# The halves of the weights begin 64 bytes later in SBUF, except for the experts

## The reference

```python
def reference(x, mem, ...):
    x = first_block(x, mem, ...)      # layer 0: RWKV-7 + S5 mixer, memory attention, SwiGLU of 2816
                                      # layer 1: differential attention, memory attention,
                                      #          8 experts of 3584, the best 2 of each token
    return second_block(x, ...)       # twice: attention + gating + convolution, then a SwiGLU of
                                      #        2816 with a convolution over tokens

def swiglu(h, w_gate, w_up, w_down):
    return (jax.nn.silu(h @ w_gate) * (h @ w_up)) @ w_down
```

## The kernel before

| tensor | first byte | modulo 256 |
|---|---|---|
| `ring` | 0 | 0 |
| `w_hi`, `w_lo` | 27648, 44032 | 0 |
| `x_hi`, `x_lo`, `act_hi`, `act_lo` | 60416, 68608, 76800, 80896 | 0 |
| `mix`, `rstd`, and `y2_hi`, `y2_lo` in `mix` | 131456, 139648 | 128 |
| `arena` (148928) with `m_hi`, `m_lo`, `d_hi`, `d_lo`, `x2_hi`, `x2_lo`, `more_hi`, `more_lo`, `more_raw`, `more_x_hi`, `sel_t`, `y_hi` | multiples of 256 behind 148928 | 192 |

## Time and profile before

### The profile page before, as it was taken

The page is one execution under the profiler, slowest core; times in us unless marked ns, Lnnn a source line. Parts: engine busy times, 40 slices in busy tenths (PEclk is TensorE's granted clock), DMA queues, the critical chain, the costliest instruction groups (busy, mean ns, idle before and its releaser), DMA issues.

```text
span 2824.1 us, 43102 instructions
## 1 busy us (share of the span) xinstructions
PE 2673.2 (95%) x18156; PEld 2377.1 (84%) x18156; DVE 1921.0 (68%) x2040; ACT 1477.4 (52%) x1687; POOL 116.2 (4%) x112
## 2 busy tenths in 40 slices
PE   7778999998998999999998899999999999999998
PEld 5667999988897887888886678888888899999998
DVE  7885656656745445875447876588888678766877
ACT  5314554456643334664336655467777565446543
POOL 7251000000000000000000000000000000000000
PEclk9899999999998999999999999999999999999999
DMA  5102545543424545885546875589999535534553
GB/s 206 61 2 92 163 155 189 194 150 105 149 75 171 191 174 196 302 321 195 180 176 255 332 278 211 214 304 351 353 342 362 205 130 182 188 116 143 193 181 120
DMA packets 219856, 558.31 MB, mean 198 GB/s; under 512 B 8592, under 2 KB 167440, under 8 KB 176400
## 3 DMA queue, kind: packets, MB, share of 16 engines
q1 hardware_dynamic: 217584, 553.47, 55.2%
q10 hardware_dynamic: 2080, 2.10, 0.2%
HBM read 554.48 MB, written 1.05 MB: 197 GB/s over the span
## 4 chain that ended last, share of the span: by engine, by line
PE 80%; DVE 9%; ACT 4%; issue 2%; DVEq 2%; DMA 1%; POOL 0%; POOLq 0%; ACTq 0%; SPq 0%
PE ps L886 23%; PE ps L888 23%; PE ps L887 22%; DVE w_lo L3508 2%; DVE w_lo L1853 2%; PE ps L1701 1%; PE ps L1702 1%; DVE more_lo L3508 1%; PE ps L1678 1%; ACT arena L1822 1%; DVEq L2608 1%; PE ps L1721 1%; ACT w_hi L1837 1%; PE ps L924 1%; PE ps L1129 1%
## 5 line engine op out<-in xcount | busy, mean ns | idle before, releaser
L1853 DVE TENSOR_TENSOR w_lo<-ring,w_hi 128x1024 fp32r<-128x1024 f32 x362 | 447.4, 1252 | 254.2 <-ACT w_hi L1837 248.2
L1837 ACT ACTIVATE w_hi<-ring 128x1024 fp32r<-128x1024 f32 x362 | 379.8, 1058 | 371.8 <-PE ps L888 356.2
L3508 DVE TENSOR_TENSOR w_lo<-ring,w_hi 128x2048 fp32r<-128x2048 f32 x168 | 384.0, 2289 | 173.7 <-ACT w_hi L1825 173.4
L886 PE MATMUL ps<-x_hi,w_hi 128*128 128x256 f32 x1600 | 459.3, 287 | 16.0 <-DVE w_lo L1853 7.9
L887 PE MATMUL ps<-x_lo,w_hi 128*128 128x256 f32 x1600 | 453.6, 284 | 0.0
L888 PE MATMUL ps<-x_hi,w_lo 128*128 128x256 f32 x1600 | 453.6, 283 | 0.0
L1825 ACT ACTIVATE w_hi<-ring 128x2048 fp32r<-128x2048 f32 x168 | 321.4, 1915 | 210.2 <-PE ps L888 135.8
L886 PEld LDWEIGHTS ps<-x_hi,w_hi 128*128 128x128 f32 x1600 | 308.0, 193 | 22.3 <-issue 16.3
L887 PEld LDWEIGHTS ps<-x_lo,w_hi 128*128 128x128 f32 x1600 | 308.3, 193 | 0.4
L888 PEld LDWEIGHTS ps<-x_hi,w_lo 128*128 128x128 f32 x1600 | 308.0, 192 | 0.0
L3508 DVE TENSOR_TENSOR more_lo<-ring,more_hi 128x2048 fp32r<-128x2048 f32 x84 | 192.4, 2290 | 87.6 <-ACT more_hi L1825 86.8
(11 more groups left out here) (451 smaller groups left out, 5832.4 us busy)
## 6 DMA issues: line engine op xcount, KB each, us to landing
ring<-moe SPq DMA_DIRECT2D x252, 1024.0 KB, 5.6
more_raw<-moe SPq DMA_DIRECT2D x84, 1024.0 KB, 5.2
ring<-ffn_w_up SPq DMA_DIRECT2D x44, 1024.0 KB, 5.1
ring<-ffn_w_down SPq DMA_DIRECT2D x22, 1024.0 KB, 4.8
ring<-xa_w_kv SPq DMA_DIRECT2D x16, 1024.0 KB, 5.3
ring<-w_in SPq DMA_DIRECT2D x16, 1024.0 KB, 5.5
ring<-da_w_qkv SPq DMA_DIRECT2D x12, 1024.0 KB, 5.1
ring<-ff_w_gate SPq DMA_DIRECT2D x11, 1024.0 KB, 5.4
```

What stands on the lines that cost most here:

```text
L886: mm(o, lhs[0], rhs[0], start=start, stop=False)
L1837: nc.scalar.activation(w_hi[:, half_slot(at, half), :], ring[:, s_, half * 1024:half * 1024 + 1024], ACT.Copy).then_inc(hi_ready, 1)
L1853: nc.vector.tensor_tensor(w_lo[:, i, :], ring[:, s_, half * 1024:half * 1024 + 1024], w_hi[:, i, :], ALU.subtract).then_inc(lo_ready, 1)
L3508: nc.vector.tensor_tensor(lo, raw_piece(n), hi, SUB).then_inc(piece_lo, 1)
```

## The change

Before `w_hi` a tensor of 16 columns (64 bytes) is put in and behind `w_lo` one of 240 columns (960 bytes). So `w_hi` and `w_lo` begin 64 bytes later, and all that follows 1024 bytes later. `even_hi` and `even_lo` are second names on the same memory, at the places where `w_hi` and `w_lo` lay before, and `split_piece`, which only the experts use, takes those.

```diff
@@ -340,8 +340,13 @@
         ring = sb("ring", [P, RING, KT * 288])
 
 
+        even_at = nc.sbuf_base
+        sb("odd_start", [P, 16])
         w_hi = sb("w_hi", [P, HALVES, 1024], F32R)
         w_lo = sb("w_lo", [P, HALVES, 1024], F32R)
+        sb("odd_end", [P, 240])
+        even_hi, even_lo = (nc.alloc_sbuf_tensor_at(f"even_w{i}", [P, HALVES, 1024], F32R, offset=even_at + 16384 * i)
+                            for i in range(2))
         x_at = nc.sbuf_base
         x_hi = sb("x_hi", [P, KT, S], F32R)
         x_lo = sb("x_lo", [P, KT, S], F32R)
@@ -490,7 +495,7 @@
         def split_piece(n):
             b = n % SPLITS
             if b < 2:
-                return [t[:, 2 * b:2 * b + 2, :].rearrange("p a n -> p (a n)") for t in (w_hi, w_lo)]
+                return [t[:, 2 * b:2 * b + 2, :].rearrange("p a n -> p (a n)") for t in (even_hi, even_lo)]
             return [t[:, b - 2, :] for t in (more_hi, more_lo)]
```

## The result

The change makes the kernel faster by 0.5%: 2815.32 us (median of 6 runs, 2804.52 to 2820.6) against 2827.85 us for the kernel before, timed beside it (6 runs, 2825.61 to 2831.57), ratio 0.995, 95% interval 0.9938 to 0.9961. The predicted 2802.5 us was 13 us too low; the range held. The six times lie 16 us apart (2820.6, 2815.04, 2813.66, 2815.59, 2815.96, 2804.52), those of before 6 us. The profiled execution is the slowest of the six, 2820.6 us, with a span of 2818.9 us and a clock of 0.978 as before.

A forecast was written before the change was run, and what follows sets the result against it. PE was taken as the bound (busy 95%), through the spacing of split-product matmuls. Gains of 36.5 us less losses of 13.3 us made 23.2 us off 2825.76 us: 2802.5 us, range 2787 to 2819.

The forecast's parts named there:

- Addresses matter at all: Split products on PE: where tiles begin sets matmul spacing, about 6.6 ns; rival "nothing at all", 2826 us, chance 0.04.
- Distance modulo 256: Split products: first byte streamed minus first byte loaded, modulo 256, sets spacing: 0 gives 120 ns, 192 113.4, 64 118.
- 118 ns everywhere: Rival: the new pairs run like w with m; gains 12.3 us, losses 13.3, 2826.8 us, no change; chance 0.10.
- `x` and `act` with `w` in the second block's feed-forwards at 113.4 ns, 20.9 us: Second block's two feed-forwards: distance 0 to 192 takes 3168 matmuls from 120.0 to 113.4 ns, gaining 20.9 us.
- slower rhythm in part: Rival: long feed-forward runs at distance 192 fall into 118 ns; one gives 2809.5 us, both 2816.5; chance 0.12.
- Distance 128 at 120 ns: m, d, x2 with w and w with m move to distance 128, taken at 120 ns: losses of 13.3 us.
- Gains in the first feed-forward and the first memory attention: Outside the second block's feed-forwards: act in the first feed-forward gains 3.5 us, 1920 matmuls of x elsewhere 11.5 us.
- Splits and experts unchanged: Splits on DVE and ACT stay at 2289 and 1915 ns, the experts' stretch at 1380 us; nothing counted.
- PE waits for nothing new: Second block's feed-forward: with PE at 179 us DVE is busy 83% and keeps ahead, so no new wait.
- The Trainium skill's rule: TensorE waits for no other SBUF user and weight loads take no read bandwidth, so addresses would be free; forecast followed rows instead.

The follow-up runs named there:

- e8: Kernel before with the arena alone moved 64 bytes later, so all pairs of split products have distance 0: 2828.01 us, ratio 0.9997.
- e4: The change with w_hi and w_lo 128 bytes later instead of 64 (x and act with w at distance 128): 2827.64 us, ratio 0.9998.
- e3: The change plus the arena 64 bytes later (m, d, x2 with w at distance 192, more with x and act at 0): 2801.96 us, ratio 0.9909.
- e11: The change with w_hi and w_lo 192 bytes later instead of 64 (x and act with w at distance 64): 2827.1 us, ratio 0.999.
- e10: e3 plus sixteen spare matmuls that load and stream w_hi in all three feed-forwards: 2799.59 us, ratio 0.9891.
- e9: The change plus sixteen spare matmuls that load and stream w_hi in the second block's two feed-forwards: 2808.62 us, ratio 0.993.
- e5: The change plus sixteen spare matmuls that load and stream x in the second block's two feed-forwards: 2820.53 us, ratio 0.9973.
- e6: e3 plus sixteen spare matmuls of distance 0 (x with x, m with m) in all three feed-forwards: 2816.12 us, ratio 0.9959.
- e7: The change without its exception: the experts' split_piece takes w_hi and w_lo at the new place too: 2816.88 us, ratio 0.9955.

## Why the prediction was right or wrong

- **Addresses matter at all: right.** It was the step on which all hung; e8 and e4 show it with the code unchanged.
- **Distance modulo 256: right in the main.** 0 gives 120.0 alone (e8), 128 gives 118.7 or 120.0 (e4), 192 gives 113.4 or 117.8 (after, e3). That 64 and 192 differ was read from too few rows: 64 gives 117.8 in all long runs, but 113.5 in one of 190 matmuls (e11), so the two differ only in how often each rhythm comes. "118 ns everywhere" is refuted by 376 to 394 us after.
- **The step that failed: `x` and `act` with `w` in the second block's feed-forwards at 113.4 ns, 20.9 us.** In the profiled execution they were at 117.8, worth 3168 x 2.2 = 7.0 us. Mechanism as in the rival *slower rhythm in part* (both feed-forwards, 2816.5), which was given 0.12; the median is 2815.3. I had seen both rhythms of distance 192 in `x2`, at one place of the code in two layers, and still read the slow layer as the exception. Two rows at one place, one of each kind, were thin ground for a chance of 0.12. The fastest execution, 2804.5, is near the forecast, but it has no profile, so whether one or both were at 113.4 in it stays open.
- **Distance 128 at 120 ns: a size that was off.** In the change it is 118.7 in nearly all runs (after). The losses come to 1440 x 5.3 = 7.6 us for `m` instead of 9.5, 1.0 for `d` instead of 1.3, and with `x2` (1.2) and `w` with `m` (0.3) to 10 us instead of 13.3.
- **The sum, done again:** 36.5 - 13.9 = 22.6 us of gains, 10 of losses, 2825.8 - 12.6 = 2813 us; median 2815.3. The profiled execution is 7 us above that, 4 of them in the experts, whose part varies by 8 us between kernels with the same places there. Runs of `x` with `w` that fell into 117.8 outside the feed-forwards (824 to 841 us) are in the rest.
- **Gains in the first feed-forward and the first memory attention: right.** 1368 matmuls in 160 us, where one third at 113.4 and two thirds at 118.7 make 116.9 ns or 1371; `x` at 113.5 from 376 to 394 us.
- **Splits and experts unchanged: right** (2290, 1914, 390 ns). The prediction took the experts' place as fixed; that `more` at distance 192 costs the experts some 10 us was in the earlier trace rows and was not used.
- **PE waits for nothing new: right.** The one wait for `w_lo` near the end of a feed-forward was there before, 2.3 us, and is 2.6 in e10, the fastest kernel.
- **The Trainium skill's rule.** SBUF — State Buffer, Who interferes with whom, has TensorE wait for no other user. No run speaks against that sentence by itself, since what was moved here is TensorE's own two operands against each other. The prediction followed the rows against the conclusion that places are therefore free, and the runs agree with the rows (in the first feed-forward 120.0 ns in e8 for 116.0 in the kernel before). They do not show whether the matmul's reads meet its successor's load or something else.

## What to carry to other kernels

Where matmuls follow one another without idle time, measure their spacing (stretch over count) for each pair of tiles, not the shown duration, and compare pairs of one shape: 6% lay here in where the tiles begin, and moving a second area with the first gained 0.4% on top of the first's 0.5%, though alone it gained nothing. If one pair shows two spacings, don't forecast the better one for a long run; count it at the worse until a run shows otherwise. Look for a distance's rhythms in all stages, the short ones too: the second rhythms of 64 and 128 stood in a stage that the long stretches leave out. A single profiled execution tells one draw: read the spread of the times as well, and look where the stages end before a difference of a few us is put down to an edit.

## What the runs showed of the hardware

- 256 streamed columns, 128 loaded, granted clock 1.00 (2.4 GHz), split products back to back: 120.0 ns at distance 0 (before, e8); 117.8, seldom 113.4, at 64 (e11); 118.7, at times 120.0, at 128 (e4); 113.4 or 117.8 at 192 (after, e3). Distance is as above, modulo 256 bytes of a partition; only multiples of 64 were tried.
- A rhythm, once taken, lasts: 1191 matmuls in 140 us or 1238, through changes between `x` and `act`, until PE halts or the distance changes (e11 and e9, the stretches of 140 us).
- Sixteen matmuls at 120 ns ahead of a run of distance 192 decide which of the two it takes, by which operand moves at the step: the streamed one 113.4 (five of five, e9 and e10), the loaded one 117.8 (five of five, e5 and e6).
- With 512 streamed columns distance 0 is the best of those seen: 227.4 ns (e3) against 229.1 at 64 (e7) and 233.4 at 192 (before). The experts' part is 1371 us with `more` at 0 and 1381 with `more` at 192.
